# Latent attention in a two-block hybrid model: its norm, scaling and key rotation placed into later attention steps, its products one step later

## The reference

```python
def mla_attention(c_q, c_kv, k_rope, q_norm, w_uq, kv_norm, w_ukv):
    pos = jnp.arange(S)
    q = (rms_norm(c_q, q_norm) @ w_uq).reshape(B, S, MLA_HEADS, MLA_NOPE + MLA_ROPE)
    q = jnp.concatenate([q[..., :MLA_NOPE], rope(q[..., MLA_NOPE:], pos)], axis=-1)
    kv = (rms_norm(c_kv, kv_norm) @ w_ukv).reshape(B, S, MLA_HEADS, MLA_NOPE + MLA_V)
    k_r = jnp.broadcast_to(rope(k_rope[:, :, None, :], pos), (B, S, MLA_HEADS, MLA_ROPE))
    k = jnp.concatenate([kv[..., :MLA_NOPE], k_r], axis=-1)
    return causal_block_attention(q, k, kv[..., MLA_NOPE:])
```

## Time and profile before

| | |
|---|---|
| median of 3 runs | 1758.55 us (1758.08 to 1759.15) |
| the profiled execution, its own time | 1759.41 us |
| its span, first to last instruction | 1757.6 us |
| TensorE busy | 1657.3 us, 94% |
| VectorE, ScalarE, GpSimd busy | 57%, 41%, 36% |
| mean granted TensorE clock | 0.976 of full speed |

### The profile page before, as it was taken

How to read it: one execution, slowest core, us unless ns; L and a number is a source line. 1 busy time by engine, 2 the same in 40 slices (tenths; PEclk the granted TensorE clock), 3 DMA queues, 4 the chain that set the end, 5 groups by cost and what they waited for, 6 DMA issues and landing times.

```text
span 1757.6 us, 34120 instructions
## 1 busy us (share of the span) xinstructions
PE 1657.3 (94%) x15054; PEld 1524.0 (87%) x15054; DVE 1008.5 (57%) x1611; ACT 718.1 (41%) x1120; POOL 629.9 (36%) x510
## 2 busy tenths in 40 slices
PE   7999999899999999998999969999999799999997
PEld 7878998899979888987999869999998698999986
DVE  3255467677773355376777766673334658652346
ACT  3444444445344444444444444522223445432223
POOL 0644673000306535653000322415545206144541
PEclk9999999999999999999999989999999899999999
DMA  7522345687455322474776544534233344432322
GB/s 283 179 97 81 126 135 224 253 286 275 168 174 187 126 92 97 144 275 171 259 275 214 197 144 144 180 99 142 91 105 121 120 168 144 157 121 98 116 79 108
DMA packets 44147, 283.55 MB, mean 161 GB/s; under 512 B 5160, under 2 KB 5288, under 8 KB 14176
## 3 DMA queue, kind: packets, MB, share of 16 engines
q1 hardware_dynamic: 42336, 272.23, 43.9%
q0 software_dynamic: 1664, 9.15, 1.4%
HBM read 280.30 MB, written 1.06 MB: 160 GB/s over the span
## 4 chain that ended last, share of the span: by engine, by line
PE 82%; DVE 8%; POOL 5%; ACT 3%; issue 1%; DMA 0%; SPq 0%; POOLq 0%; DVEq 0%; ACTq 0%
PE ps L532 79%; PE ps L540 3%; POOL part0l L2745 2%; POOL part1l L2745 2%; DVE part1l L1269 1%; DVE gates L2006 1%; DVE Xl L1284 1%; DVE part0l L1269 1%; ACT part1h L2272 1%; ACT Xh L2272 1%; ACT part0h L2272 0%; DMA hid<-in_xT 0%; ACT gates L2269 0%; POOL x L2780 0%; POOL x L2782 0%
## 5 line engine op out<-in xcount | busy, mean ns | idle before, releaser
L532 PE MATMUL ps<-Xh,part0h 128*128 128x256 f32 x1080 | 318.8, 295 | 9.9 <-DVE Xl L1284 8.2
L2272 ACT ACTIVATE part0h<-ring 128x1024 fp32r<-128x1024 f32 (+2 forms) x218 | 216.3, 1041 | 268.1 <-PE ps L532 254.8
L2272 ACT ACTIVATE part1h<-ring 128x1024 fp32r<-128x1024 f32 x218 | 216.2, 1040 | 240.1 <-PE ps L532 239.3
L532 PE MATMUL ps<-Xl,part0h 128*128 128x256 f32 x1080 | 311.0, 288 | 0.0
L532 PE MATMUL ps<-Xh,part0l 128*128 128x256 f32 x1080 | 310.7, 288 | 0.0
L532 PE MATMUL ps<-Xh,part1h 128*128 128x256 f32 x984 | 287.0, 292 | 4.7 <-DVE Xl L1284 2.9
L2745 POOL TENSOR_TENSOR part1l<-ring,part1h 128x512 fp32r<-128x512 f32 x178 | 231.4, 1332 | 153.5 <-ACT part1h L2272 153.5
L2745 POOL TENSOR_TENSOR part0l<-ring,part0h 128x512 fp32r<-128x512 f32 x170 | 224.4, 1352 | 170.0 <-ACT part0h L2272 170.0
L532 PE MATMUL ps<-Xl,part1h 128*128 128x256 f32 x984 | 280.4, 285 | 0.0
L532 PE MATMUL ps<-Xh,part1l 128*128 128x256 f32 x984 | 280.1, 285 | 0.0
L532 PEld LDWEIGHTS ps<-Xh,part0h 128*128 128x128 f32 x1080 | 212.9, 197 | 19.3 <-issue 8.4
(11 more groups left out here) (405 smaller groups left out, 3274.0 us busy)
## 6 DMA issues: line engine op xcount, KB each, us to landing
ring<-in_w SPq DMA_DIRECT2D x214, 1024.0 KB, 5.0
hid<-in_ada SPq DMA_DIRECT2D x36, 512.0 KB, 6.4
hid<-in_w SPq DMA_DIRECT2D x6, 1024.0 KB, 10.6
rows<-in_lnrow POOLq DMA_DIRECT2D x6, 1024.0 KB, 7.9
fqk<-in_ada SPq DMA_DIRECT2D x6, 512.0 KB, 6.3
cq<-in_ada SPq DMA_DIRECT2D x6, 512.0 KB, 6.1
gates<-in_c SPq DMA_DIRECT2D x2, 1536.0 KB, 7.2
plain<-in_w SPq DMA_DIRECT2D x2, 1024.0 KB, 7.2
```

The costliest lines, as they stand in the source:

```text
L532: return e.matmul(o, a, b, start=st, stop=sp)
L2272: return e.activation(o, a, ACT.Copy)
```

## The change

VectorE's `mla_norm` becomes `mla_keys(l, i)` for one row tile; the addition of epsilon and the keys of row tile 0 are done in a new job "mla0" of step 0 of attention n, those of row tile 1 in "mla1" of step 1. ScalarE's `mla_norm` is cut in two: the sums of squares stay between f and n, the scaling is done in "mla1". The jobs "latents", "up" and "turn" move from steps 2, 4 and 6 to 3, 5 and 7. Within a step they stand before h0, before h1 and before kc. GpSimd's and SyncE's programs are as before; TensorE has nothing in mla0 and mla1.

```diff
@@ def fills(l):
-             "n": "cmpk.0|cmpk.1|cmpv.0 latents|cmpv.1 h0|g0_0.0 a0 up|g0_0.1 h1|g0_1.0 a1 turn|g0_1.1 kc|g0_2.0 cs0|g0_2.1 cT0|"
+             "n": "cmpk.0 mla0|cmpk.1 mla1|cmpv.0|cmpv.1 latents h0|g0_0.0 a0|g0_0.1 up h1|g0_1.0 a1|g0_1.1 turn kc|g0_2.0 cs0|g0_2.1 cT0|"
@@ VectorE
-    def mla_norm(l):
-        w.wait_ge(*at["sumsq", l])
-        e.tensor_scalar(small[:, 36:40], small[:, 32:36], 1e-6, None, ALU.add).then_inc(*V("cvar", l))
+    def mla_keys(l, i):
         after("c1")
-        for i in range(2):
-            r = M.misc[:, i, 0:32].unsqueeze(1)
-            rope(l, r, r, i, 1)
-            w.wait_ge(*V.now())
-            e.tensor_copy(M.K4[:, i, :, 64:96], r.to_broadcast([128, 4, 32])).then_inc(*V("k4", i, l))
+        r = M.misc[:, i, 0:32].unsqueeze(1)
+        rope(l, r, r, i, 1)
+        w.wait_ge(*V.now())
+        e.tensor_copy(M.K4[:, i, :, 64:96], r.to_broadcast([128, 4, 32])).then_inc(*V("k4", i, l))
@@ VectorE, job1
+        elif name[0:3] == "mla":
+            if name == "mla0":
+                w.wait_ge(*at["sumsq", l])
+                e.tensor_scalar(small[:, 36:40], small[:, 32:36], 1e-6, None, ALU.add).then_inc(*V("cvar", l))
+            mla_keys(l, int(name[3]))
@@ VectorE, mixer
         attention(l, "f")
-        mla_norm(l)
@@ ScalarE
-    def mla_norm(l):
+    spans = ((0, 384, 384), (384, 512, 128))
+
+    def latent_squares(l):
         w.wait_ge(*at["cq0", l])
         w.wait_ge(*at["cq1", l])
-        spans = ((0, 384, 384), (384, 512, 128))
...
+
+    def latent_rows(l):
         w.wait_ge(*at["crstd", l])
         for i in range(2):
             for m, (a, b, n) in enumerate(spans):
@@ ScalarE, job1
+        elif name == "mla1":
+            latent_rows(l)
@@ ScalarE, mixer
         attention(l, "f")
-        mla_norm(l)
+        latent_squares(l)
         attention(l, "n")
```

## The result

The changed kernel takes 1750.54 us (median of 5 runs, 1748.53 to 1751.18) against 1758.08 us (5 runs) of the kernel before: a ratio of 0.9956, 95% interval 0.9945 to 0.9968, so 7.5 us or 0.44% faster. A second set of 5 runs, beside the experiments, gave 1749.38 us and 0.9954 (0.9942 to 0.9967). The forecast was 1746.8 us in a range of 1742.5 to 1751.0. The profiled execution took 1750.5 us, span 1748.8. The measured time lies within the stated range, above the band of 1745.0 to 1749.3 that the prediction gave its likeliest case.

What follows compares the result with a forecast made beforehand. TensorE, busy 94% of the span, was taken to bound the kernel. Terms of 13.0 - 0.4 - 0.9 = 11.7 us gained gave a forecast of 1746.8 us, range 1742.5 to 1751.0.

Steps and rivals of the forecast that it cites:

- likeliest case: Whole kernel: the forecast itself holds, time between 1745.0 and 1749.3 us, chance 0.60.
- large term (1): Start of attention n: `soften` of unit 0 no longer waits behind `mla_norm`; 13.0 us gained over two layers.
- rival B: Keys in mla1: GpSimd's split holds four VectorE operations, TensorE waits up to 4.2 us, clock drops; in full 1761.0, chance 0.04.
- halfway case of B: Keys in mla1: two operations held, no clock drop, TensorE waits 1.4 us; 1749.2 us, chance 0.06.
- rival D: Start of attention n: only the idle goes, half clock stays behind another small wait; 1752.1 us, chance 0.08.
- (2) mla0: VectorE, step 0: `soften` of unit 1 is 2.1 us late, but scores of unit 2 keep 0.7 us slack; cost nothing.
- Rival C: Attention n: the gap moves to the scores of unit 2 as mla0 awaits the squares; 1758.5 us, chance 0.04.
- (3) ScalarE: Squares stay before unit 0, scaling moves behind the split of g0_0 with 3 us slack; cost nothing.
- (4) mla1: VectorE, step 1: one key operation held by GpSimd, TensorE waits 0.2 us; 0.4 us lost for two layers.
- (5) The banks: Step 7: 0.73 us stall goes, waits of 1.0 at kc and 0.2 at vc come; 0.9 us lost in two layers.
- Rival A: Later in the program: clock drops after waits change; one fewer gives 1743.7, one more 1749.9 us; chance 0.18.

Runs made afterwards that it cites:

- norm_only: Changed kernel with latents, up and turn back in steps 2, 4 and 6; norm, scaling and keys as changed: 1747.2 us, ratio 0.9937.
- steps_only: Kernel before with only latents, up and turn one step later; norm, scaling and keys stay between attentions f and n: 1759.0 us, ratio 1.0007.
- scale_early: Changed kernel with ScalarE's scaling of the latents back ahead of attention n, VectorE as changed: 1753.33 us, ratio 0.9975.
- key_late: Changed kernel with the keys of row tile 1 moved from step 1 to step 6, where GpSimd has no split: 1747.17 us, ratio 0.9937.
- keys_locked: Changed kernel with the keys of both row tiles in step 1 and only the addition of epsilon in step 0: 1759.91 us, ratio 1.0006.
- kc_first: Changed kernel with kc ahead of turn in step 7: 1749.35 us, ratio 0.9951.
- after_again: The changed kernel as it is, measured once more on the same chip for comparison: 1749.38 us, ratio 0.9954.
- both: Changed kernel with key_late and kc_first together, keys of tile 1 in step 6 and kc ahead of turn: 1747.59 us, ratio 0.9938.

## Why the prediction was right, and where its sum was off

The mechanism of the large term held, the range held, and the forecast time was missed by 3.7 us. The prediction's own sign for rival B appeared, too: rotation operations over 1 us with TensorE waiting for the copy of line 1390. Its halfway case of B (1749.2, chance 0.06) comes nearer to the measured 1750.54 than the forecast. That the time still lies in the range is owed to the range's reach towards rival D, since the case that came about was thought unlikely.

**The bound and the large term (1): right.** `soften` of unit 0 starts at 92.38 and the wait at the scores of unit 1 is gone with its half clock. cmpv.0 came 6.30 us earlier relative to the start of n; 6.3 was forecast. norm_only has this gain without the later products, steps_only has the later products without this gain, and scale_early has most of it with `soften` freed alone.

**(2) mla0: right.** It ends at 97.4, `soften` of unit 1 right behind it, and TensorE does not wait at unit 2 (98.51). Rival C is out.

**(3) ScalarE: right.** The scaling ran from 101.01 to 102.70, wanted at 107.51. What it would cost to leave the scaling before n was not priced; scale_early shows a wait of 2.0 us a layer for it.

**(4) mla1: the mis-sized term.** The prediction took "one operation (the copy into K4, which starts after 101.3) as held": 0.2 us a layer. The place and the mechanism were right and the count was not: two were held, and the wait is 1.30 us a layer. With 0.96 us added to the times of the trace after, to set its start of attention n on that of the trace before, the split was to start at 101.34 and started at 101.19, and the fourth operation begins at 101.23, 0.04 us behind it. An estimate 0.15 us off was worth 1.1 us, since the fourth operation was then held for a whole GpSimd instruction and the copy into K4 for the next. Two layers: 2.2 us. The prediction's halfway case of B, two operations held, had the wait right (1.4) but no drop of the clock; in layer 2 there was one, for 1.5 us. Together 3.7 us, close to the 3.6 between the 11.7 us forecast and the 8.06 gained in attention n. key_late and scale_early, where no operation is held, and keys_locked, where four are, show the cause.

**(5) The banks: right.** 0.73 us went. In layer 1 the wait at kc is 0.98 us, and vc starts 0.39 us behind kc where the kernel before needed 0.24 for it, so 0.15 more; in layer 2 the wait is 0.89 and vc 0.24 later. That is 1.13 us in each and 0.40 lost, as forecast. That the bank is g0_1's is shown by kc_first; that the 0.73 us came from the bank of the first turned queries rests on the count and on its going with the order of the products.

**Rival A, the clock elsewhere: it exists, and it limits what can be gained.** In the changed kernel's profile it cost nothing (the rest took 1058.92 us against 1058.81). In key_late's it cost 1.9 us, though the program is the same there, and the clock isn't. The stretch of 800 to 840 us in the changed kernel and in key_late (columns as in the earlier trace rows):

```profile
800.00:840.00 40.00, 35.20 (x282) 31.82 (x281) 26.83 (x46) 19.58 (x33) 2.69 (x4) 0.91 0.66 248
```

```profile
800.00:840.00 40.00, 35.24 (x258) 32.69 (x255) 28.54 (x46) 19.32 (x29) 1.11 (x2) 0.87 0.68 264
```

Waits of the same length, 4.5 us earlier (a wait of 2.10 us before 813.98 in the changed kernel, before 809.53 in key_late), are followed by more of the 1.2 GHz level: 0.87 in place of 0.91 over 40 us is 3.2 us more at half speed, or 1.6 us lost. The rule of the Trainium skill (TensorE: Matmul & The Clock Gate, "Part 1: The HAM clock gate"), that the activity count runs freely and the number of slow products depends on its phase, agrees with this, and with the equal waits of 1.30 us: a drop followed in layer 2 of the changed kernel and none in its layer 1, and none in either layer of kc_first.

**Rival B** in full, as keys_locked has it, ends at 1759.9 us, where its full case stood at 1761.0. **Rival D**, half clock behind some other small wait, occurred in part: behind the wait of 1.30 us in layer 2, for 1.5 us of its 5.3.

**A slip.** The prediction speaks of places changed "in five queues' programs"; the diff changes three, TensorE's, VectorE's and ScalarE's.

The distances of the other profiles, as in the table above:

| kernel | to n, layer 1 | n, layer 1 | to n, layer 2 | n, layer 2 | rest |
|---|---|---|---|---|---|
| after_again | 90.88 | 100.69 | 395.47 | 102.22 | 1058.84 |
| steps_only | 90.60 | 104.77 | 395.01 | 105.85 | 1058.27 |
| keys_locked | 90.98 | 106.51 | 395.64 | 106.13 | 1058.84 |
| norm_only | 92.36 | 99.87 | 394.91 | 99.91 | 1060.15 |
| key_late | 91.70 | 99.38 | 394.91 | 99.36 | 1060.75 |
| kc_first | 91.20 | 100.19 | 395.65 | 100.19 | 1060.97 |
| both | 91.90 | 98.82 | 396.58 | 98.82 | 1060.38 |
| scale_early | 92.12 | 103.06 | 396.63 | 101.58 | 1060.81 |

Open: norm_only, key_late and both differ in attention n (99.9, 99.4 and 98.8 us a layer) and not in the whole time beyond the spread of their runs (1747.20, 1747.17 and 1747.59 us). That the clock in the rest takes the difference back is read from one profile of each; why it is at half speed for longer there was not settled.

## What to carry to other kernels

Look at what stands in an engine's queue ahead of the read that frees a PSUM bank: 3.8 us of small work in that place cost over 6 us a layer, and behind the read most of it was hidden. Before putting small operations between SBUF tiles on VectorE into a new place, find GpSimd's instructions there: each held one of them here, for up to its whole length, so a tenth of a us in the place was worth over 1 us, and a step in which GpSimd has nothing is worth a search. A gain under 0.2% is best read from the distances of the stage that was changed, since the clock elsewhere moved the whole time by as much. When TensorE's order is moved, count the PSUM banks through `take` and `give` again, since each product inherits the readers of another.

## What the runs showed of the hardware that was not expected

One GpSimd instruction held one VectorE operation each time. In layer 1 of keys_locked these took 1.11, 1.32, 1.17 and 1.30 us against 0.17 to 0.19 alone, and in both layers there were four for GpSimd's four instructions. Not every operation was caught: in layer 1 VectorE's next operation was held again each time, in layer 2 two of them passed in 0.18 and 0.16 us.

Nor was every kind of operation. VectorE's instruction of line 1406, which reads PSUM and one SBUF tile, takes 0.41 us at 103.22 in the changed kernel, under GpSimd's split, and 0.42 without one. The maximum of line 1410, which reads one SBUF tile and writes another, takes 0.42 us at 103.67 under the same split and as much outside one, so that "from SBUF to SBUF", as the prediction puts it, is too wide. The Trainium skill (SBUF — State Buffer, "Practical consequences") has the rule, that the pair is held for the whole instruction; the runs add how many operations that catches.

What followed a wait was not a matter of its length alone. Waits of 1.30 us were followed by a drop of the clock in layer 2 and by none in layer 1, in both profiles of the changed kernel. kc_first has the same wait at the same place in layer 2 (before 599.07 us, in after_again before 599.06), and there the clock stayed up. In scale_early the equal waits of 1.99 and 2.00 us went the other way round: granted clock 0.72 over 101 to 107 us, 1.00 over 600 to 607.
